# Norms in token form in the rounds, and a ring of three score buffers in the heads

## What is computed

```python
kk = heads(k * k_k)
kk = kk / jnp.maximum(jnp.sqrt(jnp.sum(kk * kk, axis=-1, keepdims=True)), 1e-12)
...
mean = jnp.mean(wkv, axis=-1, keepdims=True)
var = jnp.mean(jnp.square(wkv - mean), axis=-1, keepdims=True)
y = ((wkv - mean) * lax.rsqrt(var + GN_EPS)).reshape(B, S, RWKV_WIDTH) * ln_w + ln_b
```

```python
s = jnp.einsum('bqgrd,bkgd->bgrqk', qi, k).astype(jnp.float32) * scale
p = jax.nn.softmax(s, axis=-1).astype(v.dtype)
return jnp.einsum('bgrqk,bkgv->bqgrv', p, v)
```

## Time and profile before

| | us |
|---|---|
| median of 3 runs (2863.75 to 2866.16) | 2863.81 |
| the profiled execution | 2862.11 |
| its span, first to last instruction | 2860.3 |
| TensorE busy / VectorE / ScalarE / GpSimd | 2600.9 / 1240.2 / 1085.9 / 809.8 |
| mean granted clock of TensorE | 0.966 |
| the four rounds | 471 to 1052 |
| heads of the first layer / of the second | 2123.5 to 2328 / 2624.8 to 2788 |

### The profile page before, as it was taken

The page is one execution under the profiler, slowest core; times in us unless marked ns, Lnnn a source line. Parts: engine busy times, 40 slices in busy tenths (PEclk is TensorE's granted clock), DMA queues, the critical chain, the costliest instruction groups (busy, mean ns, idle before and its releaser), DMA issues. The chain is left out here.

```text
span 2860.3 us, 49221 instructions
## 1 busy us (share of the span) xinstructions
PE 2600.9 (91%) x19266; PEld 2041.7 (71%) x19266; DVE 1240.2 (43%) x1839; ACT 1085.9 (38%) x1682; POOL 809.8 (28%) x342
## 2 busy tenths in 40 slices
PE   8999979989898979888999999989978888998987
PEld 6887857868686857776778887767855566776665
DVE  3222024455655537344242220055846642584652
ACT  4443224343434323553233442233344422335441
POOL 3444433313232313112434444412210002232002
PEclk9999989999999989999999999999999999999998
DMA  4232322212121212111423233311110001121001
GB/s 135 90 95 92 105 66 86 91 52 83 59 83 59 83 39 74 52 38 59 134 82 95 88 95 98 100 37 53 55 41 1 1 9 51 52 74 59 1 1 66
DMA packets 52005, 188.49 MB, mean 66 GB/s; under 512 B 5760, under 2 KB 6016, under 8 KB 51712
## 3 DMA queue, kind: packets, MB, share of 16 engines
q1 hardware_dynamic: 50688, 181.74, 20.3%
q10 hardware_dynamic: 1152, 4.26, 0.4%
HBM read 183.88 MB, written 2.10 MB: 65 GB/s over the span
## 5 line engine op out<-in xcount | busy, mean ns | idle before, releaser
L2392 POOL TENSOR_TENSOR WLO<-RAW,WHI 128x1024 fp32r<-128x1024 f32 x334 | 804.7, 2409 | 2010.5 <-ACT WHI L299 2010.5
L299 ACT ACTIVATE WHI<-RAW 128x1024 fp32r<-128x1024 f32 x336 | 355.8, 1059 | 999.7 <-PE psum L313 708.8
L311 PE MATMUL psum<-HHI,WHI 128*128 128x512 f32 x872 | 353.8, 406 | 40.2 <-DVE HLO L397 15.0
L312 PE MATMUL psum<-HLO,WHI 128*128 128x512 f32 x872 | 347.0, 398 | 0.0
L313 PE MATMUL psum<-HHI,WLO 128*128 128x512 f32 x872 | 346.6, 397 | 0.0
L311 PE MATMUL psum<-H2HI,WHI 128*128 128x512 f32 (+1 forms) x536 | 197.3, 368 | 32.5 <-DVE H2LO L395 23.0
L311 PEld LDWEIGHTS psum<-HHI,WHI 128*128 128x128 f32 x872 | 165.8, 190 | 84.0 <-issue 43.9
L312 PEld LDWEIGHTS psum<-HLO,WHI 128*128 128x128 f32 x872 | 165.9, 190 | 41.7 <-issue 3.4
L313 PEld LDWEIGHTS psum<-HHI,WLO 128*128 128x128 f32 x872 | 165.7, 190 | 39.6
L312 PE MATMUL psum<-H2LO,WHI 128*128 128x512 f32 (+1 forms) x536 | 191.6, 357 | 0.0
L313 PE MATMUL psum<-H2HI,WLO 128*128 128x512 f32 (+1 forms) x536 | 191.2, 357 | 0.0
(11 more groups left out here) (394 smaller groups left out, 5196.6 us busy)
## 6 DMA issues: line engine op xcount, KB each, us to landing
RAW<-in_wstream SPq DMA_DIRECT2D x336, 512.0 KB, 3.5
X<-in_xT SPq DMA_DIRECT2D x8, 256.0 KB, 7.3
out_T<-OUT SPq DMA_DIRECT2D x4, 512.0 KB, 2.6
W3S<-in_lora ACTq DMA_DIRECT2D x5, 384.0 KB, 3.1
XC<-in_ctxT ACTq DMA_DIRECT2D x1, 1024.0 KB, 5.6
TRIG<-in_trig ACTq DMA_DIRECT2D x1, 960.0 KB, 7.6
FCC<-in_first SPq DMA_DIRECT2D x1, 576.0 KB, 9.0
LVL<-in_levels SPq DMA_DIRECT2D x1, 384.0 KB, 9.3
```

The lines of the kernel that those rows point to most:

```text
L299: act.activation(WHI[:, q % 2, :], RAW[:, q % 2, :], ACT.Copy).then_inc(rounded, 1)
L311: pe.matmul(out, tile_of(WHI, slot, u), hi(kt), start=first and last[0], stop=False)
L312: pe.matmul(out, tile_of(WHI, slot, u), lo(kt), start=False, stop=False)
L2392: pool.tensor_tensor(WLO[:, s, :], RAW[:, s, :], WHI[:, s, :].bitcast(F32), ALU.subtract)\
```

## The change

**Token form.** `kkss` and `var` become `token_sums`: for each block of 128 tokens the squares are the weights and the two columns of `heads` the moving side, so that the sums come out with tokens on the partitions, 128x2 for a block, 128x8 for a set. Root, maximum and reciprocal run on 128x8 in the new tile `ROOT`. `spread` (`kkb`, `varb`) brings them back over the 64 rows of each head: eight products with a broadcast column of `ROOT` as weights and the identity as moving side, into `B[0]`, from which `kk` and `n0` now read. `kkb` stands between streamed blocks 1 and 2, `varb` behind the last streamed block; `low_ranks(p)` of the next round waits for `n0_p`; both small maxima and reciprocals stand ahead of `unit_key(0)`; both `rinv` ahead of `n0_0`; `e3` doesn't wait for `kk`.

**Heads.** Scores go round three PSUM pairs, and run two units ahead; the transposes share one pair (`TURNED`), so they wait for the copy of the unit before. ScalarE copies all 768 columns and takes the exponential of `u + 1` ahead of that copy; VectorE has no copy, and one reciprocal for a pair. The value products of a pair lie in the last 256 columns of the buffer of `sc(2j + 1)`, which the scores two pairs' units later need: for even units the scores are split, 512 columns first, then values and transposes, and the last 256 columns when `y` has been read.

```diff
+        ROOT = ra("ROOT", [P, 2, 2 * BLOCKS])
...
-                    pe.wait_ge(*A.before(f"sd_{p}", i))
-                    pe.wait_ge(*V.before(f"dd_{p}", i))
+                    pe.wait_ge(*V.before(f"n0_{p}", i))
...
+                def token_sums(name, p, src, *waits):
+                    for w in waits:
+                        pe.wait_ge(*w)
+                    for b in range(BLOCKS):
+                        mm = pe.matmul(SETS[p].B[0][:, 2 * b:2 * b + 2], src[:, b * P:(b + 1) * P], two_heads, start=True, stop=True)
+                    mm.then_inc(*S.inc(f"{name}_{p}"))
+                def spread(name, p, *waits):
+                    for w in waits:
+                        pe.wait_ge(*w)
+                    pe.sem_inc(tensor_ready)
+                    for b in range(BLOCKS):
+                        for h in range(2):
+                            mm = pe.matmul(SETS[p].B[0][h * HD:(h + 1) * HD, b * P:(b + 1) * P],
+                                           ROOT[:, p, 2 * b + h:2 * b + h + 1].to_broadcast([P, HD]), eye, start=True, stop=True)
+                    mm.then_inc(*S.inc(f"{name}_{p}"))
                 def tokens(p):
 
                     d = SETS[p]
                     pe.wait_ge(*V.at(f"ktl_{p}", i))
-                    pe.wait_ge(*A.at(f"kkn_{p}", i))
...
-                    head_sums("kkss", p, SETS[p].B[0], SETS[p].E1[:, :], A.at(f"kksq_{p}", i))
-                whole(streamed(1), streamed(2))
+                    token_sums("kkss", p, SETS[p].E1, A.at(f"kksq_{p}", i))
+                whole(streamed(1))
+                for p in TWO:
+                    spread("kkb", p, V.at(f"kkinv_{p}", i))
+                whole(streamed(2))
                 head_sums("bonus", 0, SETS[0].B[1], SETS[0].RK[:, :], V.at("rk_0", i))
                 whole(streamed(3))
...
-                    head_sums("var", p, SETS[p].B[0], SETS[p].DSQ[:, :], A.at(f"dsq_{p}", i))
+                    token_sums("var", p, SETS[p].DSQ, A.at(f"dsq_{p}", i))
                 whole(tail)
+                for p in TWO:
+                    spread("varb", p, V.at(f"rinv_{p}", i))
...
-                    run("e3", p, d.E3[:, :], d.SG[:, :], ACT.Exp, V.at(f"cprev_{p}", i), V.at(f"kk_{p}", i), scale=-DECAY)
+                    run("e3", p, d.E3[:, :], d.SG[:, :], ACT.Exp, V.at(f"cprev_{p}", i), scale=-DECAY)
...
-                    run("kkn", p, d.E3[:, :], d.B[0], ACT.Sqrt, S.at(f"kkss_{p}", i))
+                    run("kkn", p, ROOT[:, p, :], d.B[0][:, 0:2 * BLOCKS], ACT.Sqrt, S.at(f"kkss_{p}", i))
...
-                    run("sd", p, SETS[p].E1[:, :], SETS[p].B[0], ACT.Sqrt, S.at(f"var_{p}", i), scale=1.0 / HD, bias=EPS[:, 1:2])
+                    run("sd", p, ROOT[:, p, :], SETS[p].B[0][:, 0:2 * BLOCKS], ACT.Sqrt, S.at(f"var_{p}", i), scale=1.0 / HD, bias=EPS[:, 1:2])
...
+                def unit_root(p):
+                    ts(f"kkmax_{p}", ROOT[:, p, :], ROOT[:, p, :], 1e-12, None, ALU.max, None, A.at(f"kkn_{p}", i))
+                    inverse(f"kkinv_{p}", ROOT[:, p, :], V.at(f"kkmax_{p}", i))
                 def unit_key(p):
                     d = SETS[p]
-                    ts(f"kkmax_{p}", d.E3[:, :], d.E3[:, :], 1e-12, None, ALU.max, None, A.at(f"kkn_{p}", i))
-                    inverse(f"kkinv_{p}", d.E3[:, :], V.at(f"kkmax_{p}", i))
-                    stt(f"kk_{p}", d.KK[:, :], d.RKV[:, 1, :], col("k_k", i * 2 + p), d.E3[:, :], ALU.mult, ALU.mult, V.at(f"kkinv_{p}", i))
+                    stt(f"kk_{p}", d.KK[:, :], d.RKV[:, 1, :], col("k_k", i * 2 + p), d.B[0], ALU.mult, ALU.mult, S.at(f"kkb_{p}", i))
...
+                unit_root(0)
+                unit_root(1)
                 unit_key(0)
...
+                    inverse(f"rinv_{p}", ROOT[:, p, :], A.at(f"sd_{p}", i))
+                for p in TWO:
                     d = SETS[p]
                     dv = d.DV[:, :]
-                    inverse(f"rinv_{p}", d.E1[:, :], A.at(f"sd_{p}", i))
-                    tt(f"n0_{p}", dv, dv, d.E1[:, :], ALU.mult, V.at(f"rinv_{p}", i))
+                    tt(f"n0_{p}", dv, dv, d.B[0], ALU.mult, S.at(f"varb_{p}", i))
...
+        SCORES, TURNED = (two_banks[0], two_banks[1], two_banks[3]), two_banks[2]
...
-            def scores(u):
+            def scores(u, ps):
                 kind, i, a, qb = us[u]
-                if u >= 2:
-                    pe.wait_ge(*A.at(f"ex{u - 2}"))
-                pe.sem_inc(tensor_ready)
...
-                    mm = pe.matmul(two_banks[a][:, at:at + w], lhs, rhs, start=True, stop=True)
-                mm.then_inc(*S.inc(f"sc{u}"))
+                    mm = pe.matmul(SCORES[u % 3][:, at:at + w], lhs, rhs, start=True, stop=True)
+                if ps[-1][0]:
+                    mm.then_inc(*S.inc(f"sc{u}"))
             def values(j):
                 kind, i, _, qb = us[2 * j]
-                out = two_banks[3][:, TT:TT + 2 * P]
+                out = SCORES[(2 * j + 1) % 3][:, TT:TT + 2 * P]
...
-                pe.wait_ge(*V.at(f"ri{2 * j + 1}"))
-                for u in (2 * j, 2 * j + 1):
-                    pe.wait_ge(*V.at(f"pt{u}"))
-                    pe.wait_ge(*A.at(f"pt{u}"))
+                pe.wait_ge(*V.at(f"ri{j}"))
+                pe.wait_ge(*A.at(f"pt{2 * j + 1}"))
                 pe.sem_inc(tensor_ready)
...
-            scores(0)
-            for u, (kind, i, a, qb) in enumerate(us):
-                j = u // 2
-                if u + 1 < len(us):
-                    scores(u + 1)
-                if a == 0 and j:
-                    values(j - 1)
+            def turned(u):
+                _, _, a, qb = us[u]
                 pe.wait_ge(*A.at(f"ex{u}"))
-                if a and j:
-                    pe.wait_ge(*V.at(f"y{j - 1}"))
+                if u:
+                    pe.wait_ge(*A.at(f"pt{u - 1}"))
                 pe.sem_inc(tensor_ready)
                 for b in keys_of(qb):
-                    mm = pe.transpose(two_banks[2 + a][:, b * P:(b + 1) * P], PX[:, a, b * P:(b + 1) * P], eye)
+                    mm = pe.transpose(TURNED[:, b * P:(b + 1) * P], PX[:, a, b * P:(b + 1) * P], eye)
                 mm.then_inc(*S.inc(f"tr{u}"))
+            PARTS2 = ((0, T), (T, TC))
+            scores(0, PARTS2)
+            scores(1, PARTS2)
+            for u in range(len(us)):
+                j, ahead = u // 2, u + 2 < len(us)
+                if ahead:
+                    if u:
+                        pe.wait_ge(*A.at(f"ex{u - 1}"))
+                    pe.sem_inc(tensor_ready)
+                    scores(u + 2, PARTS2 if u % 2 else PARTS2[:1])
+                if j and u % 2 == 0:
+                    values(j - 1)
+                turned(u)
+                if ahead and u % 2 == 0:
+                    if j:
+                        pe.wait_ge(*V.at(f"y{j - 1}"))
+                    pe.sem_inc(tensor_ready)
+                    scores(u + 2, PARTS2[1:])
             values(len(us) // 2 - 1)
...
+            def exponent(u):
+                kind, _, a, qb = us[u]
+                c0 = 0 if qb < BLOCKS else T
+                act.wait_ge(*V.at(f"nm{u}"))
+                if u >= 2:
+                    act.wait_ge(*S.at(f"tr{u - 2}"))
+                act.activation(PX[:, a, c0:], SCORES[u % 3][:, c0:TT], ACT.Exp, scale=scale_of(kind), bias=NM2[:, u % COLS:u % COLS + 1],
+                               accum_out=DEN2[:, u % COLS:u % COLS + 1]).then_inc(*A.inc(f"ex{u}"))
...
+            exponent(0)
             for u, (kind, i, a, qb) in enumerate(us):
                 j = u // 2
                 c0 = 0 if qb < BLOCKS else T
...
+                if u + 1 < len(us):
+                    exponent(u + 1)
+                if a and j:
+                    rounded_part(j - 1)
                 act.wait_ge(*S.at(f"tr{u}"))
                 if j:
                     act.wait_ge(*S.at(f"pv{j - 1}"))
-                if qb < BLOCKS:
-                    act.activation(PTS[:, a, 0:T], two_banks[2 + a][:, 0:T], ACT.Copy).then_inc(*A.inc(f"pt{u}"))
-                else:
-                    act.sem_inc(A.inc(f"pt{u}")[0])
-                if a and j:
-                    rounded_part(j - 1)
+                act.activation(PTS[:, a, c0:], TURNED[:, c0:TT], ACT.Copy).then_inc(*A.inc(f"pt{u}"))
             rounded_part(len(us) // 2 - 1)
...
-            def inverse(u):
-                dve.wait_ge(*A.at(f"ex{u}"))
-                dve.reciprocal(DEN2[:, u % COLS:u % COLS + 1], DEN2[:, u % COLS:u % COLS + 1]).then_inc(*V.inc(f"ri{u}"))
...
             def result(j):
+                out = SCORES[(2 * j + 1) % 3]
                 dve.wait_ge(*S.at(f"pv{j}"))
...
             largest(0)
-            for u, (kind, i, a, qb) in enumerate(us):
+            largest(1)
+            for u in range(len(us)):
                 j = u // 2
-                if u:
-                    inverse(u - 1)
-                if u + 1 < len(us):
-                    largest(u + 1)
-                dve.wait_ge(*S.at(f"tr{u}"))
-                if j:
```

(19 more changed lines are left out.)

56 lines of the change are left out of this document (23 added, 33 removed).

## The result

| | before | after |
|---|---|---|
| median, us | 2863.8 (2854.6 to 2866.2, 4 runs) | 2824.3 (2823.5 to 2828.9, 4 runs) |
| ratio, with its 95% interval | | 0.9883 (0.9867 to 0.9898) |
| profiled execution / its span | 2862.1 / 2860.3 | 2828.9 / 2827.1 |
| VectorE / ScalarE / TensorE busy | 1240 / 1086 / 2601 | 1126 / 1107 / 2601 |

The ratio is the one on record. The two medians divided give 0.9862; in later batches the median of before was 2858.1, 2859.9 and 2861.7, so the gain lies between 33 and 40 us.

A forecast was written before the change was run, and what follows sets the result against it. TensorE was taken as near its limit in rounds and heads, so only its idle time, started by VectorE, could be won. Rounds -7.8 and heads -4.5 us from the median 2863.8 gave 2851.5, range 2841 to 2865.

The forecast's parts named there:

- The wait for the squares goes, with the bonus and token waits: Rounds 2 to 4: TensorE's 5.83 us wait for the key's squares and 1.46 for the bonus vanish; tokens' 1.62 becomes 0.15.
- The spreads cost 0.9 each: Rounds, TensorE: each new spread of eight products takes 0.9 us, four in a round 3.7; bounds 0 and 2.2 each.
- D: Slower case: spreads whose loads don't overlap cost 1.3 us more each, giving 2870, or 2877 with half of C's ring; chance 0.12.
- VectorE's chain through the turn: Turn into round 2: GpSimd holds `n2_0` until 612.05; `yf_1` ends at 615.85, before at 620.70; `csum_1` at 630.9.
- B: Key norm: GpSimd asks after the scan has ended and comes behind `cprev_1`; 2842.8 us, chance 0.13, margin 0.1 us.
- "TensorE meanwhile starts `low_ranks(0)` at 609.8 to 610.6": Turn into round 2: TensorE starts one or two us later than now and reaches the squares' sums at 622.1.
- "Here the new wait sits": Key norm, rounds 2 to 4: GpSimd delays `cprev_1`, so TensorE waits 4.7 us for `kkinv_0`, plus 1.5 for lower clock.
- The state products: Rounds, first state product to end of the tail: the prediction had no term, so a change of 0.
- The end of round 4, -4.9: End of round 4: VectorE's alone, 4.9 us shorter; its spreads hide in the 13.7 us wait, which becomes 8.9.
- Heads, -4.5: Both layers' heads: -1.5 us over 48 full pairs, -1.0 at a layer's end, -0.5 at its start; -4.5 in all.
- ring: Heads: chain from one pair's values to the next sets the pace, 6.38 us a pair, or 6.48 for 64 rows.

The follow-up runs named there:

- token form alone: Kernel before with only the token form of both norms in the rounds, heads as before: median 2831.9 us, ratio 0.9902.
- The fifth run: Kernel before with 64 empty waits on TensorE ahead of the sums of the key's squares: 2861.0 us, ratio 0.9998.
- heads-alone run: Kernel before with only the new order of the heads, rounds as before: median 2846.9 us, ratio 0.9952.

## Why the forecast was wrong, by its own steps

- **The wait for the squares goes, with the bonus and token waits**: right. All are 0 in the change.
- **The spreads cost 0.9 each**: 0.98 (1.97 for two). Right, with D out.
- **VectorE's chain through the turn**: right. Counted from the last tail product, `yf_1` was to end at 8.2 and ended at 8.4, `csum_1` at 23.2 and 23.4. The instruction opened to the block was `n1_0`, a `tensor_scalar` with a single input in SBUF, and not `n2_0` (1.95 us for 0.55). So the form that I named under B for `kkmax` does meet GpSimd, one step earlier. At the end of the chain that changes next to nothing (0.2 us).
- **"TensorE meanwhile starts `low_ranks(0)` at 609.8 to 610.6" and has the squares' sums at 622.1**: this step failed. In the same count that is 2.1 to 2.9 and 14.4 us; measured are 4.9 and 17.9. I let only `n0_0` hold the start. The turn of the loop, whose waits of 1.0 to 1.3 us the trace of before showed, and which the short spreads no longer cover, takes 3.0, and low clock behind it 1.6 more (13.0 us up to the sums, and 11.4 in the two rounds of the token form alone that had none).
- **"Here the new wait sits"**, 4.7 us and 1.5 for the clock, three times, 18.6 in all: measured 0, and 1.25 us twice in the token form alone. It fell with the step above. The subtraction of GpSimd that was to meet `cprev_1` follows TensorE, came at 26.7 and not at 23.1, and missed it; and TensorE itself reached the spreads 3.6 us later, when both reciprocals were done. That is B's mechanism, to which I had given 0.13; I saw that timing decides, but put the margin at 0.1 us, and it was 3.2. B's own time, 2842.8, still lies 18.5 above the result. With VectorE 2.2 us later the wait was 5.07.
- **The state products**: no term, and with 8.3 us the largest miss in the rounds. Four stalls, 4.7 us, and some 2.5 us of low clock behind the one of round 1 went, and about 1 us in shorter pieces. The fifth run gets 8.0 of it by place alone. The row of waits with "issue" behind it stood in the profile of before, and I let it lie as if nothing in the edit could touch it.
- **The end of round 4, -4.9**: -4.4. From the end of the tail to the next stage it is 9.3 us for 13.7, since the reciprocals are done before the tail ends. TensorE's wait in it is 7.4, because the two spreads fill 1.9; the 8.9 that I named as the wait left them out.
- **Heads, -4.5**: ring 6.38 (128 rows) and 6.48 (64 rows) forecast, 6.43 and 6.42 measured, the copy 0.80 for the 0.83 between its bounds; -5.3 in the two stretches. Right. The 5.6 us behind them, through the clock, were no term.

The sum: of the 21 us that were missing, 14 lie in the rounds and 5.6 behind the heads. The rounds divide like this (before, after, difference, and what the terms of the forecast say for the same part):

| part of the rounds | before | after | difference | forecast |
|---|---|---|---|---|
| start of round 1 to its bonus product | 24.5 | 28.1 | +3.7 | +1.9 |
| end of the tail to the next bonus product, three turns | 104.5 | 99.8 | -4.7 | +1.2 |
| bonus product to first state product, four rounds | 340.7 | 332.8 | -7.9 | -6.0 |
| first state product to end of the tail, four rounds | 97.5 | 89.1 | **-8.3** | 0 |
| end of the tail of round 4 to the next stage | 13.7 | 9.3 | -4.4 | -4.9 |

The step on the turn is the second row. There the 18.6 us of wait and low clock weren't paid, but TensorE came 3.5 us later to the squares' sums of every round, so that 5.9 us are left of it. The state products, put at nothing, make 8.3. In the first row the change's clock was low for 3.4 us from 472.3 on, and that of before wasn't.

The two parts don't quite add: 0.9902 and 0.9952 make 0.985 and the change has 0.988. By stages 3.8 us of that lie in the rounds, where the clock fell behind all three turns of the change's profiled execution and behind one of the token form's. A fall can be there in one profile and not in another with the same instructions: the heads-alone run has 13.1 us up to the squares' sums of round 1, before 11.4. What decides it stays open.

## What to carry over

Walk every engine that sets when another one asks: the collision hung on two engines' times against each other, and an error of 3.6 us on one side turned a wait of 5 us into none. Treat a wait for nothing on record as a term: find out whether it sits with a place in the program or a jump, since an edit that adds or shortens instructions moves it. Put products with many columns ahead of a loop's turn, and keep an engine's side work (`hi`) off the ring that sets the pace.

## What the runs showed of the hardware

- TensorE's instructions come in loads of 16 KB, and their place in the program alone makes or removes stalls of 0.5 to 1.7 us where short records follow each other. Sixty-four empty instructions ahead of them took 8.0 us off the four rounds' stretches behind the first state product, and cost 10.1 in round 1.
- At a loop's turn TensorE went on 2.7 to 3.2 us after the start of a load there, whether that load started 0.1, 1.5 or 2.6 us ahead of the last product's end (3.5 to 4.4 in the kernels with the rounds of before, which have two loads there). Six products of 512 columns behind the short ones took 1.1 to 1.8 us off the wait. The operation that the profile names as releaser there needn't be one that the product waits for.
- A `tensor_scalar` with one input in SBUF meets GpSimd's subtraction as well: 2.18 us for 0.16 (128x8), 1.95 for 0.55 (128x512). Here GpSimd held VectorE up until its own instruction ended, however small VectorE's was: the 128x8 ended 0.02 us after it, the `tensor_scalar` of 128x512 0.28, `v_1` with two inputs in SBUF 0.54.
- An idle piece of TensorE is paid twice where the clock falls behind it (it does not always): 236 equal products took 58.4 us of busy time at a mean clock of 0.88 and 53.7 at 0.93.
